# Expert rows gated at the store and gathered with accumulating transfers into the residual, in a two-layer MoE encoder

## The chip, the core and the metric

The kernel runs on one core of one Trainium2 chip, as one launch. The metric is the device time of the launch in microseconds (us), the median of several executions.

## What is computed

Two post-norm layers on x of 512 tokens by 1024 in float32. Each layer is `h = LN(alpha*h + mixer(h))` and then `h = LN(alpha*h + MoE(h))`. The mixer of the first layer is a retention and an RG-LRU head group, that of the second a gated linear recurrence (HGRN2), whose first step is a projection to v. The MoE is what the change touches:

```python
probs = softmax(x @ router_w)                       # 16 experts in 4 groups
# every token picks one group and the top-2 experts in it; gates = their probabilities, normalised
hid = silu(xblk @ w_gate[e]) * (xblk @ w_up[e])     # 1024 -> 512
yb  = hid @ w_down[e]                               # 512 -> 1024
y   = zeros.at[buf_tok].add(yb * buf_gate)          # two gated expert rows are added for each token
h   = _layer_norm(DN_ALPHA * h + y, ln_w, ln_b)
```

## The kernel before, in words

All engines run hand-ordered programs that are joined by semaphores. SyncE (queue q1) issues the weight loads, ScalarE (queue q10) the stores of expert rows, GpSimd (queue q0) the indirect transfers. `h` holds the residual in SBUF as four tiles (t = 0 to 3) of 128 tokens by 1024. `ps` is all of PSUM, eight banks of 512.

**Routing** (`route`, VectorE): the top-2 choice gives each token two slots, `dst[:, t, k]`, k = 0 and 1, and two gates, `gts`. The slots fill ten units of 128 rows (NU = 10, the last one is LAST). VectorE builds `lane_sel` and `token_of`; TensorE multiplies them (`rows_of_slots`, L652, placed after the first ten matmuls of unit 0's gate product) and VectorE turns the result into `row_at`, the token of each slot, by which GpSimd gathers the units' input rows.

**Units** (`moe`): for each unit TensorE does a gate, an up and a down product; ScalarE copies the 128 rows of the down product from PSUM to `yo` (L1102, in the helper L970) and stores them to `slot_rows` in DRAM (L1104). The last unit's rows stay in SBUF, `y_last`. Rounds for extra units stand in the program and are skipped when routing needs none; in this execution none ran. GpSimd multiplies h by alpha early in the MoE (`h_scaled`).

**End of a MoE.** When the ninth unit's rows are in DRAM (`y_stored`), GpSimd issues eight indirect gathers (L1872) of 128 rows by 4 KB, two for each tile, into the buffers `Yg`. VectorE (`norm_moe`) waits for a tile's two gathers, and adds each to h with its gate (L1471, L1473; `merged`). TensorE then sums each tile in PSUM: h through an identity matrix (L776) and the last unit's rows through the gated selection matrix `last_selT` (L781; `summed`). VectorE takes the statistics of a tile (L1413 to L1416), ScalarE the root (L1080), VectorE scales and shifts (L1427, L1431).

**After the first MoE** the v projection (L827) needs two things: the transposed tiles of h, and the two 2 MB halves of its weights, `w_v1`, which SyncE loads (L410) once the last tile's gathers have landed (`gathered[NT - 1]` at 32). TensorE waits for both halves before its first matmul. **After the second MoE** the normed tiles are stored as the output.

Of the kernel before, what the change touches and what calls it, by code (L numbers as in the profile page):

```python
# [15 lines left out]
ALU = mybir.AluOpType  # L16
# [3 lines left out]
P = 128  # L20
# [100 lines left out]
def encoder_kernel(nc, x, w_in_even, w_out_even, lru_conv_w, lru_conv_b, lru_gate_w, lru_gate_b,  # L121
# [3 lines left out]
    with ExitStack() as ctx:  # L125
# [20 lines left out]
        gts = sb("gts", [P, NT, 2])  # L146
        tbl = sb("tbl", [1, 32], I32)
# [75 lines left out]
        in_unit, past, token_of, lane = (scratch[:, 2048 + 80 * n:2128 + 80 * n] for n in range(4))  # L223
        yo = [scratch[:, 2048 + 1024 * n:3072 + 1024 * n] for n in range(2)]
        Yg = [[W3(20480, NT, D), W3(12288, NT, D)], [S3(8192, NT, D), S3(0, NT, D)]]
# [26 lines left out]
        r_rel, r_in, r_f1, r_first = (r_(2 * NT) for _ in range(4))  # L252
        r_lg = r_x
        last_sel = rt[:, 0:T].rearrange("p (t n) -> p t n", t=NT)
        last_selT, last_tmp = rt[:, T:2 * T], rt[:, T:T + P]
# [31 lines left out]
        h_scaled, merged, summed = sem("h_scaled"), sem("rows_merged"), sem("last_rows_summed")  # L287
# [44 lines left out]
        def _(sp):  # L332
# [44 lines left out]
            def moe_loads(L):  # L377
# [78 lines left out]
        def _(pe):  # L456
# [167 lines left out]
            def moe(L):  # L624
# [13 lines left out]
                def turned_extra_rows(j):  # L638

                    pe.wait_ge(extra_sel[L], j * 3 + 3)  # L640
# [327 lines left out]
        def _(act):  # L968
# [113 lines left out]
            def moe(L):  # L1082
# [13 lines left out]
                def store(b, k, stores=None):  # L1096

                    if stores is not None:
                        act.wait_ge(y_stored[L][k], stores)
                    for half in range(2):  # L1100
                        act.wait_ge(down_mm[L], b * 2 + half + 1)
                        copy(yo[k][:, half * 512:(half + 1) * 512], ps[:, 2 + half, :]).then_inc(y_copied[L], 1)  # L1102
# [12 lines left out]
                sigmoid(1)  # L1115
                store(0, 0)
# [7 lines left out]
                for half in range(2):  # L1124
                    act.wait_ge(down_mm[L], LAST * 2 + half + 1)
                    copy(y_last[:, half * 512:(half + 1) * 512], ps[:, 2 + half, :]).then_inc(y_copied[L], 1)
                act.wait_ge(table_done, 2 * L + 2)
                rounds = act.value_load(tbl[0:1, T_ROUNDS:T_ROUNDS + 1], min_val=0, max_val=ROUNDS)
                with act.Fori(0, ROUNDS, 1) as r:
                    with act.If(r < rounds):  # L1130
                        with act.Fori(0, PER_ROUND, 1) as i:
                            j = r * PER_ROUND + i
                            sigmoid(j + NU)
                            store(j + NU, 0, (j + NU // 2) * 16)
# [106 lines left out]
        def _(dve):  # L1241
# [163 lines left out]
            def tile_of(n, t):  # L1405

                halves = h[:, t, :].rearrange("p (a n) -> p a n", a=2)
                return halves, ps[:, 2 * t:2 * t + 2, :] if n % 2 else halves
# [56 lines left out]
            def norm_moe(L):  # L1465

                for t in range(NT):
                    dve.wait_ge(gathered[t], (L + 1) * 32)
                    if t == 0:
                        dve.wait_ge(h_scaled, L + 1)  # L1470
                    done(v.scalar_tensor_tensor(h[:, t, :], Yg[L][t // 2][:, 2 * (t % 2), :], gts[:, t, 0:1], h[:, t, :],  # L1471
                                                ALU.mult, ALU.add))
                    v.scalar_tensor_tensor(h[:, t, :], Yg[L][t // 2][:, 2 * (t % 2) + 1, :], gts[:, t, 1:2], h[:, t, :],  # L1473
                                           ALU.mult, ALU.add).then_inc(merged, 1)
                for t in range(NT):
                    dve.wait_ge(summed, L * NT + t + 1)
                    statistics(2 * L + 1, t)
# [454 lines left out]
```

## Time and profile before

| what | value |
|---|---|
| median of 3 runs | 1285.65 us (1285.23 to 1286.3) |
| span of the profiled execution | 1281.6 us |
| TensorE busy / VectorE busy | 96% / 41% of the span |
| chain that ended last | PE 79%, DMA 10%, DVE 7% |
| end of the first MoE, from the first gather's issue to the first v matmul | 504.43 to 535.75 us |
| end of the second MoE, from the first gather's issue to the end of the span | 1240.20 to 1281.6 us |

The profile is of one execution, whose own device time is not listed beside its span; the span is 4.05 us less than the median of the runs, which lies around it (launch and end). A busy share is an average over stages; the chain says which work ended last in each.

### The profile page before, as it was taken

How to read it: one execution, taken by the hardware profiler on the slowest of the kernel's cores; microseconds unless marked ns; L12 is line 12 of the kernel's file. 1: busy time of each engine (PE TensorE's matmuls, PEld its weight loads, DVE VectorE, ACT ScalarE, POOL GpSimd, SP SyncE). 2: the span in 40 equal slices, each digit the busy share in tenths (PEclk: the TensorE clock that was granted, in tenths of full speed). 3: DMA queues.
4: the chain of work that ended last, by engine and by line, in shares of the span. 5: the costliest groups of instructions: out<-in, count | busy, mean ns of one | idle time of the engine just before them, and what ended most of it. 6: DMA issues, size and time to landing. Idle time of an engine off the chain costs nothing.

```text
span 1281.6 us, 13883 instructions
## 1 busy us (share of the span) xinstructions
PE 1229.9 (96%) x5503; PEld 572.1 (45%) x5503; DVE 524.5 (41%) x1028; ACT 187.3 (15%) x315; POOL 168.5 (13%) x129
## 2 busy tenths in 40 slices
PE   8999999989999998999999999999899899999995
PEld 4444465443333333444555555555454433333332
DVE  1542693472211110700465766566625822111118
ACT  0016510110000000111111111111112200000000
POOL 0000310004000001000122323233310040000020
PEclk9999999999999999999999999999999999999998
DMA  9900074269999999553220122100045699999993
GB/s 355 359 1 0 1 279 185 94 265 368 425 428 426 429 428 423 223 146 131 66 66 17 50 66 65 50 15 1 1 176 250 263 411 422 430 425 429 426 415 125
DMA packets 77233, 292.62 MB, mean 228 GB/s; under 512 B 6420, under 2 KB 46200, under 8 KB 64760
## 3 DMA queue, kind: packets, MB, share of 16 engines
q1 hardware_dynamic: 59872, 257.30, 50.5%
q10 hardware_dynamic: 12408, 16.67, 3.6%
q0 software_dynamic: 4896, 17.83, 3.6%
q8 instruction: 43, 0.70, 0.2%
q14 instruction: 14, 0.11, 0.0%
HBM read 269.24 MB, written 22.54 MB: 228 GB/s over the span
## 4 chain that ended last, share of the span: by engine, by line
PE 79%; DMA 10%; DVE 7%; issue 1%; POOL 1%; ACT 1%; DVEq 0%; SPq 0%; POOLq 0%
PE ps L673 16%; PE ps L840 15%; PE ps L502 11%; PE ps L708 9%; PE ps L579 7%; PE ps L827 4%; PE ps L862 4%; DMA W<-moe_w_up 4%; PE ps L892 2%; DMA slot_rows<-hT 2%; DMA W<-moe_w_gate 2%; PE ps L629 1%; DVE S L1756 1%; PE ps L728 1%; PE ps L571 1%
## 5 line engine op out<-in xcount | busy, mean ns | idle before, releaser
L673 PE MATMUL ps<-W,S 128*64 128x512 f32 (+1 forms) x1200 | 272.8, 594 | 3.5 <-ACT S L970 1.5
L840 PE MATMUL ps<-hT,W 128*128 128x512 f32 x512 | 232.6, 593 | 0.7 <-ACT W L970 0.7
L673 PE MATMUL ps<-S 128*32 128x512 f32 (+1 forms) x592 | 140.4, 593 | 3.6 <-DMA W<-moe_w_gate 2.5
L673 PEld LDWEIGHTS ps<-W,S 128*64 128x64 f32 (+1 forms) x1200 | 82.9, 123 | 132.5 <-issue 129.0
L840 PEld LDWEIGHTS ps<-hT,W 128*128 128x128 f32 x512 | 92.9, 191 | 90.3 <-issue 88.4
L708 PE MATMUL ps<-W,hT 128*64 128x512 f32 (+1 forms) x512 | 116.6, 605 | 3.9 <-DVE hT L1695 2.0
L1894 POOL TENSOR_TENSOR W<-S,sq 128x256 f32<-128x256 f32 x64 | 73.5, 1148 | 159.3 <-PE ps L862 115.6
L502 PE MATMUL ps<-W,hT 128*128 128x512 f32 x192 | 86.4, 609 | 2.1 <-DMA W<-w_in_even 2.1
L708 PE MATMUL ps<-S,hT 128*32 128x512 f32 (+1 forms) x384 | 86.6, 599 | 1.1 <-DVE hT L1695 1.1
L970 ACT ACTIVATE hT<-ps 128x512 f32<-128x512 f32 x68 | 39.0, 598 | 330.3 <-PE ps L708 238.5
L1798 DVE TENSOR_TENSOR S<-S 128x512 f32<-128x512 f32 x64 | 47.8, 747 | 68.1 <-PE ps L862 56.3
L862 PEld LDWEIGHTS ps<-S,W 128*128 128x128 f32 x448 | 61.3, 192 | 30.1 <-issue 30.1
L1851 POOL DMA_INDIRECT S<-token_rows,row_at x18 | 17.4, 967 | 398.4 <-DVE row_at L1618 199.1
L1686 DVE TENSOR_TENSOR hT<-hT,ps 128x512 f32<-128x512 f32 x20 | 13.7, 686 | 132.5 <-ACT hT L1094 132.5
L862 PE MATMUL ps<-S,W 128*128 128x128 f32 x448 | 63.5, 286 | 1.4 <-issue 0.8
L673 PEld LDWEIGHTS ps<-S 128*32 128x32 f32 (+1 forms) x592 | 41.8, 118 | 47.7 <-issue 47.3
L1691 DVE TENSOR_TENSOR hT<-hT,ps 128x512 f32<-128x512 f32 x20 | 13.8, 688 | 114.7 <-PE ps L673 114.7
L708 PEld LDWEIGHTS ps<-W,hT 128*64 128x64 f32 (+1 forms) x512 | 34.7, 126 | 55.9 <-issue 54.8
L1695 DVE COPY hT<-ps 128x512 f32<-128x512 f32 x20 | 13.8, 690 | 110.8 <-PE ps L697 110.8
L579 PE MATMUL ps<-S 128*128 128x512 f32 x128 | 57.7, 594 | 1.0 <-DVE S L1734 1.0
L502 PEld LDWEIGHTS ps<-W,hT 128*128 128x128 f32 x192 | 37.2, 196 | 47.8 <-issue 45.3
L970 ACT ACTIVATE W<-ps 128x512 f32<-128x512 f32 x56 | 32.6, 597 | 172.6 <-PE ps L871 46.0
(276 smaller groups left out, 1350.9 us busy)
## 6 DMA issues: line engine op xcount, KB each, us to landing
W<-moe_w_gate SPq DMA_DIRECT2D x24, 2048.0 KB, 18.6
W<-moe_w_up SPq DMA_DIRECT2D x21, 2048.0 KB, 22.7
W<-moe_w_down SPq DMA_DIRECT2D x20, 2048.0 KB, 25.9
S<-moe_w_down SPq DMA_DIRECT2D x12, 2048.0 KB, 24.9
S<-moe_w_up SPq DMA_DIRECT2D x11, 2048.0 KB, 22.2
S<-moe_w_gate SPq DMA_DIRECT2D x8, 2048.0 KB, 20.9
W<-w_in_odd SPq DMA_DIRECT2D x32, 512.0 KB, 6.3
slot_rows<-hT ACTq DMA_DIRECT2D x18, 512.0 KB, 10.5
```

What stands on the lines that cost most here:

```text
L502: last = pe.matmul(ps[:, 4 + n % 4, :], a, b, start=(c == 0), stop=(c == ND - 1))
L579: last = pe.matmul(ps[:, k, :], srcT[:, c, t * P:(t + 1) * P], w[:, c, half * 512:(half + 1) * 512], start=(start and c == tiles[0]), stop ...
L673: last = pe.matmul(ps[a:a + n, bank, :], xgT[:, c, a:a + n], home(kind, p)[:, c, :], start=(c == 0), stop=(c == ND - 1))
L708: last = pe.matmul(ps[a:a + n, 2 + half, :], hidT[:, c, a:a + n], home(DOWN, p)[:, c, half * 512:(half + 1) * 512], start=(c == 0), stop=( ...
L827: last = pe.matmul(ps[:, k, :], hT[:, c, t * P:(t + 1) * P], w_v1[c // 4][:, c % 4, (k % 2) * 512:(k % 2 + 1) * 512], start=(c == 0), stop ...
L840: last = pe.matmul(ps[:, f % 2, :], ring[slot][:, f, c, :], hT[:, c, :], start=(c == 0), stop=(c == ND - 1))
L862: last = pe.matmul(o, km[level % 2][:, c * P:(c + 1) * P], mixed(Q2, s, c * P, P), start=True, stop=True)
L892: last = pe.matmul(ps[:, 7, :], vh[:, j, :], attn[:, j, :], start=(j == 0), stop=(j == NT - 1))
L970: return nc.scalar.activation(o, i, ACT.Copy)
L1798: v.tensor_tensor(q, q, view(src, at + 1, [[2, n], [step - 1, 2], [0, s]]), ALU.mult).then_inc(updated, 1)
L1851: pool.indirect_dma_start(xg[u % 3], None, token_rows, bass.IndirectOffsetOnAxis(ap=row_at[:, u:u + 1], axis=0)).then_inc(xg_in[u % 3], 16)
L1894: pool.tensor_tensor(view(km[level % 2], s, [[4 * s, m], [s, 2], [1, s]]), view(K2, s, [[4 * s, m], [T + s, 2], [1, s]]), view(ones, 0, [[ ...
```

## The change

- GpSimd no longer gathers into buffers. Each of the eight transfers adds the rows that it reads in DRAM to a tile of `h` in SBUF (`compute_op=ALU.add`). The order is k = 0 for the four tiles, then k = 1 for the four; before a tile's second transfer GpSimd waits until its first has landed.
- The rows must therefore be gated when they are stored: ScalarE's copies get a scale per row, `gate_at`, which comes out of `rows_of_slots` as ten more columns (`held_by` holds tokens and gates). So VectorE computes the gates `gts` ahead of the selection matrices and not behind them.
- VectorE's eight merging operations are gone. In the second MoE TensorE waits for a tile's transfers and sums as before. In the first MoE TensorE only sums the last unit's rows, and VectorE adds that from PSUM to h.
- SyncE loads the first half of the v weights when the last tile's first transfer has landed, and the second half when its second has.
- The selection of the last unit's rows (`last_gates`, now `last_rows`) holds ones, and takes 9 operations of VectorE where it took 22.

```diff
@@ weights of the v projection (SyncE, first layer)
                     sp.wait_ge(gate_mm[0], NU)
-                    sp.wait_ge(gathered[NT - 1], 32)
                     for half in range(2):
+                        sp.wait_ge(gathered[NT - 1], 16 * (half + 1))
                         sp.dma_start(w_v1[half], w_in_odd[0][half * 512:half * 512 + 512, D:2 * D].rearrange(rows, p=P)
                                      ).then_inc(wout_in, 16)
@@ rows_of_slots (TensorE)
-                        last = pe.matmul(ps[:, 7, 0:NU], lane_sel[:, k, :], token_of[:, k * NU:(k + 1) * NU],
+                        last = pe.matmul(ps[:, 7, 0:2 * NU], lane_sel[:, k, :], held_by[:, k * 2 * NU:(k + 1) * 2 * NU],
                                          start=(k == 0), stop=(k == 2 * NT - 1))
@@ last sums (TensorE)
                 for t in range(NT):
-                    pe.wait_ge(merged, L * NT + t + 1)
                     if t == 1:
                         pe.wait_ge(y_copied[L], copies)
-                    for half in range(2):
-                        pe.matmul(ps[:, 2 * t + half, :], ident, h[:, t, half * 512:(half + 1) * 512],
-                                  start=True, stop=False)
+                    if L == 1:
+                        pe.wait_ge(gathered[t], 64)
+                        for half in range(2):
+                            pe.matmul(ps[:, 2 * t + half, :], ident, h[:, t, half * 512:(half + 1) * 512],
+                                      start=True, stop=False)
                     if t == 0:
                         pe.wait_ge(y_copied[L], 2 * NU)
                     for half in range(2):
                         last = pe.matmul(ps[:, 2 * t + half, :], last_selT[:, t * P:(t + 1) * P],
-                                         y_last[:, half * 512:(half + 1) * 512], start=False, stop=True)
+                                         y_last[:, half * 512:(half + 1) * 512], start=(L == 0), stop=True)
@@ store and the last unit's copies (ScalarE)
+                def gated(o, i, u):
+                    return nc.scalar.activation(o, i, ACT.Copy, scale=gate_at[:, u:u + 1])
...
-                        copy(yo[k][:, half * 512:(half + 1) * 512], ps[:, 2 + half, :]).then_inc(y_copied[L], 1)
+                        gated(yo[k][:, half * 512:(half + 1) * 512], ps[:, 2 + half, :], b if extra is None else NU
+                              ).then_inc(y_copied[L], 1)
...
+                act.wait_ge(slots_done, 2 * L + 2)
                 store(0, 0)
@@ norm_moe (VectorE)
+                if L == 0:
+                    dve.wait_ge(h_scaled, 1)
                 for t in range(NT):
-                    dve.wait_ge(gathered[t], (L + 1) * 32)
-                    if t == 0:
-                        dve.wait_ge(h_scaled, L + 1)
-                    done(v.scalar_tensor_tensor(h[:, t, :], Yg[L][t // 2][:, 2 * (t % 2), :], gts[:, t, 0:1], h[:, t, :],
-                                                ALU.mult, ALU.add))
-                    v.scalar_tensor_tensor(h[:, t, :], Yg[L][t // 2][:, 2 * (t % 2) + 1, :], gts[:, t, 1:2], h[:, t, :],
-                                           ALU.mult, ALU.add).then_inc(merged, 1)
-                for t in range(NT):
+                    if L == 0:
+                        dve.wait_ge(gathered[t], 32)
                     dve.wait_ge(summed, L * NT + t + 1)
+                    if L == 0:
+                        halves, _ = tile_of(1, t)
+                        done(v.tensor_tensor(halves, ps[:, 2 * t:2 * t + 2, :], halves, ALU.add))
                     statistics(2 * L + 1, t)
@@ route (VectorE)
                 ins.then_inc(slots_done, 1)
+                for k, (d, slot) in enumerate(slots):
+                    done(v.tensor_tensor(by_token(r_rk), by_token(d), per_token(slot), ALU.is_equal))
+                    done(v.tensor_tensor(r_rk, r_rk, r_x, ALU.mult))
+                    done(v.tensor_reduce(gts[:, :, k], by_token(r_rk), AX.X, ALU.add))
...
                 dve.wait_ge(cum_ps, 2 * L + 2)
+                v.tensor_copy(gate_at[:, 0:NU], ps[:, 7, NU:2 * NU])
                 v.tensor_copy(row_at[:], ps[:, 7, 0:NU]).then_inc(slots_done, 1)
-                for k, (d, slot) in enumerate(slots):
-                    done(v.tensor_tensor(by_token(r_rk), by_token(d), per_token(slot), ALU.is_equal))
-                    done(v.tensor_tensor(r_rk, r_rk, r_x, ALU.mult))
-                    done(v.tensor_reduce(gts[:, :, k], by_token(r_rk), AX.X, ALU.add))
@@ the gathers (GpSimd)
                 pool.wait_ge(y_stored[L][0], stores)
-                for t in range(NT):
-                    for k in range(2):
-                        pool.indirect_dma_start(Yg[L][t // 2][:, 2 * (t % 2) + k, :], None, xs,
-                                                bass.IndirectOffsetOnAxis(ap=dst[:, t, k:k + 1], axis=0)
-                                                ).then_inc(gathered[t], 16)
+                pool.wait_ge(h_scaled, L + 1)
+                for k in range(2):
+                    for t in range(NT):
+                        if k == 1:
+                            pool.wait_ge(gathered[t], 32 * L + 16)
+                        pool.indirect_dma_start(h[:, t, :], None, xs,
+                                                bass.IndirectOffsetOnAxis(ap=dst[:, t, k:k + 1], axis=0),
+                                                compute_op=ALU.add).then_inc(gathered[t], 16)
```

On GpSimd, at the end of the first MoE, the rows before (names in brackets are the semaphores waited for; `tbl` is the table of rounds):

```order
L1851 DMA S<-token_rows,row_at 128x1024 [waits xgT_in_psum_0] x6
L1866 TENSOR_LOAD tbl [waits table_done]
L1866 ISA x2
L1872 DMA W<-slot_rows,dst 128x1024 [waits y_stored0_0,y_stored0_1]
L1872 DMA W<-slot_rows,dst 128x1024 x7
L1878 MEMSET S 128x512 [waits v_copied]
```

and now:

```order
L1877 TENSOR_LOAD tbl [waits table_done]
L1877 ISA x2
L1886 DMA h<-slot_rows,dst 128x1024 [waits h_scaled,y_stored0_0,y_stored0_1]
L1886 DMA h<-slot_rows,dst 128x1024 x3
L1886 DMA h<-slot_rows,dst 128x1024 [waits gathered_0]
L1886 DMA h<-slot_rows,dst 128x1024 [waits gathered_1]
L1886 DMA h<-slot_rows,dst 128x1024 [waits gathered_2]
L1886 DMA h<-slot_rows,dst 128x1024 [waits gathered_3]
```

The eight transfers stand at the same place; the last four have got a wait each for the first transfer of the same tile.

On VectorE, in `route`, between the cast of the slots and the rows that TensorE's `rows_of_slots` waits for, before:

```order
L1591 CAST dst<-S 128x4 x2
L1598 SCALAR_TENSOR_TENSOR hT<-iota,S 128x80
L1600 TENSOR_SCALAR hT<-hT 128x80
L1601 SCALAR_TENSOR_TENSOR hT<-hT 128x80
L1602 TENSOR_TENSOR hT<-hT 128x80
L1603 TENSOR_REDUCE hT<-hT 128x8
L1604 TENSOR_TENSOR S<-iota,hT 128x1024
L1606 TENSOR_TENSOR hT<-hT,iota 128x80
```

and now, first behind the cast:

```order
L1606 CAST dst<-S 128x4 x2
L1609 TENSOR_TENSOR S<-S 128x64
L1610 TENSOR_TENSOR S<-S 128x64
L1611 TENSOR_REDUCE gts<-S 128x4
L1609 TENSOR_TENSOR S<-S 128x64
L1610 TENSOR_TENSOR S<-S 128x64
L1611 TENSOR_REDUCE gts<-S 128x4
L1617 SCALAR_TENSOR_TENSOR hT<-iota,S 128x80
```

and then at the end of that stretch:

```order
L1621 TENSOR_TENSOR hT<-hT 128x80
L1622 TENSOR_REDUCE hT<-hT 128x8
L1623 TENSOR_TENSOR S<-iota,hT 128x1024
L1627 TENSOR_TENSOR hT<-hT,iota 128x8x10
L1627 TENSOR_TENSOR hT<-hT,gts 128x8x10
L1630 TENSOR_SCALAR sm<-S 128x8
```

Seven operations more stand ahead of the semaphore `sel_done` that TensorE waits for: six that make the gates, and the product with them.

## Rows read from the trace of the kernel before

**Rows 1.** The page: its span, its first line by engine, its chain by engine.

```profile
span 1281.6 us, 13883 instructions
...
PE 1229.9 (96%) x5503; PEld 572.1 (45%) x5503; DVE 524.5 (41%) x1028; ACT 187.3 (15%) x315; POOL 168.5 (13%) x129
...
PE 79%; DMA 10%; DVE 7%; issue 1%; POOL 1%; ACT 1%; DVEq 0%; SPq 0%; POOLq 0%
```

**Rows 2.** Chain that ended last, in order of time: start us, us, what.

```profile
513.20 9.13 DMA W<-slot_rows,dst
522.84 12.87 DMA W<-w_in_odd
535.75 7.13 PE ps L827 x16
```

**Rows 3.** Timeline, end of the first MoE: start us, us, engine, line, operation.

```profile
504.43 0.95 POOL L1872 DMA_INDIRECT W<-slot_rows,dst  x1 [96.44 <-DMA slot_rows<-hT]
...
510.06 1.09 PE L708 MATMUL ps<-W,hT 128*64 128x512 f32 x1 [1.93 <-DMA S<-moe_w_down]
...
522.40 0.94 SPq L410 DMA_DIRECT2D W<-w_in_odd  x2
```

**Rows 4.** DMA queues, 507 to 508 and then 508 to 522.5 us: packets, MB, share.

```profile
q1 hardware_dynamic: 88, 0.39, 96.4%
...
q0 software_dynamic: 1152, 4.19, 72.6%
q1 hardware_dynamic: 159, 0.57, 10.0%
```

**Rows 5.** Stretches: length, busy us of PE, PEld, DVE, ACT, POOL, granted clock, DMA share, GB/s.

```profile
508.00:519.00 11.00, 9.07 (x35) 3.09 (x34) 4.87 (x5) 0.75 (x2) 4.74 (x5) 0.84 1.00 399
524.00:534.00 10.00, 9.62 (x29) 4.55 (x27) 6.76 (x12) 0.99 (x3) 0.00 (x0) 1.00 1.01 394
510.00:513.50 3.50, 3.44 (x10) 1.14 (x11) 0.00 (x0) 0.00 (x0) 2.59 (x4) 0.51 1.03 410
```

**Rows 6.** Timeline, end of the second MoE and the last norm.

```profile
1240.20 0.95 POOL L1872 DMA_INDIRECT S<-slot_rows,dst  x1 [96.47 <-DMA slot_rows<-hT]
...
1252.64 1.98 PE L776 MATMUL ps<-h,sq 128*128 128x512 f32 x4
...
1254.47 1.88 PE L781 MATMUL ps<-S 128*128 128x512 f32 x4
...
1260.19 1.29 DVE L1413 BATCH_NORM_STATS2 sm<-ps 128x6 f32<-128x512 f32 x2
...
1264.77 1.29 DVE L1413 BATCH_NORM_STATS2 sm<-ps 128x6 f32<-128x512 f32 x2
```

**Rows 7.** DMA queue q1, 1241 to 1242 and then 1242 to 1257 us.

```profile
q1 hardware_dynamic: 89, 0.43, 105.4%
...
q1 hardware_dynamic: 162, 0.57, 9.4%
```

**Rows 8.** Timeline of the routing, first layer (two rows) and second layer.

```profile
284.03 0.24 DVE L1606 TENSOR_TENSOR hT<-hT,iota 128x80 f32<-128x80 f32 x1
...
286.90 1.95 PE L652 MATMUL ps<-hT,S 128*128 128x10 f32 x16
...
1019.63 0.23 DVE L1606 TENSOR_TENSOR hT<-hT,iota 128x80 f32<-128x80 f32 x1
...
1020.81 1.95 PE L652 MATMUL ps<-hT,S 128*128 128x10 f32 x16
...
1025.69 0.35 SPq L366 DMA_DIRECT2D W<-moe_w_gate  x1
```

**Rows 9.** Single lines: durations in ns, min/median/max; then indirect DMA to landing.

```profile
L1217 ACT ACTIVATE S<-ps,sm x8: 672/687/714, 962.3 to 994.1; 128x512 f32<-128x512 f32 x8
...
L1427 DVE SCALAR_TENSOR_TENSOR h<-ps,sm,S x8: 1265/1266/1267, 527.0 to 1276.0; 128x1024 f32<-128x1024 f32 x8
...
DMA to landing us min/median/max: 5.8/7.3/9.2
```

More of the change, by code:

```diff
@@ L222, in encoder_kernel @@
         first_rows = scratch[:, 3072:4096]
-        in_unit, past, token_of, lane = (scratch[:, 2048 + 80 * n:2128 + 80 * n] for n in range(4))
+        in_unit, past, lane = (scratch[:, 2048 + 80 * n:2128 + 80 * n] for n in range(3))
+        held_by = scratch[:, 2288:2448]
         yo = [scratch[:, 2048 + 1024 * n:3072 + 1024 * n] for n in range(2)]
-        Yg = [[W3(20480, NT, D), W3(12288, NT, D)], [S3(8192, NT, D), S3(0, NT, D)]]
         y_last = xg[1]
@@ L251, in encoder_kernel @@
         r_blk = r_gt[:, 0:MAXX * NE]
-        r_rel, r_in, r_f1, r_first = (r_(2 * NT) for _ in range(4))
+        r_rel, r_f1, r_first = (r_(2 * NT) for _ in range(3))
         r_lg = r_x
         last_sel = rt[:, 0:T].rearrange("p (t n) -> p t n", t=NT)
-        last_selT, last_tmp = rt[:, T:2 * T], rt[:, T:T + P]
+        last_selT = rt[:, T:2 * T]
         T_ROUNDS, T_STORES, T_COPIES, T_ORDER = MAXX, MAXX + 1, MAXX + 2, 16
@@ L638, in turned_extra_rows @@
                 def turned_extra_rows(j):
-                    pe.wait_ge(extra_sel[L], j * 3 + 3)
+                    pe.wait_ge(extra_sel[L], j * 4 + 1)
+                    for t in range(NT):
+                        for k, sel in enumerate((first_sel, other_sel)):
+                            last = pe.matmul(ps[:, 7, 0:1], sel[:, t, :], gts[:, t, k:k + 1],
+                                             start=(t == 0 and k == 0), stop=(t == NT - 1 and k == 1))
+                    last.then_inc(extra_gates[L], 1)
+                    pe.wait_ge(extra_sel[L], j * 4 + 4)
                     for half in range(2):
@@ L1094, in sigmoid, with store @@
                     nc.scalar.activation(sig, ps[:, 0, :], ACT.Sigmoid).then_inc(sig_done[L], 1)
-                def store(b, k, stores=None):
+                def gated(o, i, u):
+                    return nc.scalar.activation(o, i, ACT.Copy, scale=gate_at[:, u:u + 1])
+                def store(b, k, stores=None, extra=None):
                     if stores is not None:
                         act.wait_ge(y_stored[L][k], stores)
+                    if extra is not None:
+                        act.wait_ge(extra_sel[L], extra * 4 + 3)
                     for half in range(2):
                         act.wait_ge(down_mm[L], b * 2 + half + 1)
-                        copy(yo[k][:, half * 512:(half + 1) * 512], ps[:, 2 + half, :]).then_inc(y_copied[L], 1)
+                        gated(yo[k][:, half * 512:(half + 1) * 512], ps[:, 2 + half, :], b if extra is None else NU
+                              ).then_inc(y_copied[L], 1)
                     act.wait_ge(y_copied[L], b * 2 + 2)
@@ L1125, in moe @@
                     act.wait_ge(down_mm[L], LAST * 2 + half + 1)
-                    copy(y_last[:, half * 512:(half + 1) * 512], ps[:, 2 + half, :]).then_inc(y_copied[L], 1)
+                    gated(y_last[:, half * 512:(half + 1) * 512], ps[:, 2 + half, :], LAST).then_inc(y_copied[L], 1)
                 act.wait_ge(table_done, 2 * L + 2)
@@ L1133, in moe @@
                             sigmoid(j + NU)
-                            store(j + NU, 0, (j + NU // 2) * 16)
+                            store(j + NU, 0, (j + NU // 2) * 16, extra=j)
             norm_std(0, 0)
@@ L1705, in moe @@
                     if u == 1:
-                        last_gates(L)
+                        last_rows(L)
                     elif u == 4:
-                        last_gates_turned(L)
+                        last_rows_turned(L)
                     elif L == 0 and u == 6:
@@ L1869, in moe @@
                 pool.wait_ge(y_stored[L][0], stores)
[L1870 to L1874 removed]
+                pool.wait_ge(h_scaled, L + 1)
+                for k in range(2):
+                    for t in range(NT):
+                        if k == 1:
[3 more added lines that the diff above has]
+                                                compute_op=ALU.add).then_inc(gathered[t], 16)
             moe(0)
```

44 lines of the change are left out of this document (20 added, 24 removed).

## The prediction, made before the changed kernel ran

> **What bounds the kernel now.** I read the page first: TensorE is busy for 96% of the span and holds 79% of the chain that ended last [rows 1]. So only what moves TensorE's start or end counts. The chain in order of time shows the two places that the change touches. At the end of the first MoE it leaves TensorE: last gather (513.20, landed 522.33), loads of the v weights (second half issued 522.84, landed 535.71), v projection at 535.75 [rows 2]. The first v matmul waits for weights, which wait for gathers; VectorE's merging is not on that path. At the end of the second MoE the chain is the gathers and then VectorE: the last norm starts at 1260.19 and each of its four tiles takes 4.58 us (1260.19 to 1264.77) [rows 6]. The third place is the routing of the second layer, where the first load of new weights is issued at 1025.69, when unit 0's gate product is done [rows 8].
>
> Then I read the queues. The first gather is issued at 504.43 and none of its bytes move before 508; 0.57 MB of weights are still to come then, and the eight gathers move 4.19 MB [rows 3, 4]. From 508 to 519 the DMA share is 1.00 at 399 GB/s [rows 5]: the transfers are bound by the DMA engines, not by GpSimd's issue (0.95 us each). One gather of 0.524 MB costs c = 0.524 / 0.399 = 1.31 us of all 16 engines. 508.1 + 0.57/0.399 (1.4) + 8 x 1.31 = 520.0, and the last one counted as landed at 522.33: 2.3 us lie between last data and release.
>
> **The change, part by part.**
>
> *The accumulating transfer* is the unknown. No row shows one. It writes the same bytes as a gather, but it must also read the tile of h. Lower bound: that read is hidden and c stays 1.31 us (factor 1). Upper bound: the read takes the engines as long as the gather itself, so c = 2.62 us (factor 2); the engines are at 1.00 already [rows 5], so there is no idle share to take it in. I take 1.5, the middle: half of the second read hidden behind the write, c = 1.96 us. I know nothing from the trace that says which half; both ends stay for the range.
>
> The Trainium skill, "Collectives: The Full Stack", section "The bandwidth ceiling: the fold count and why AG ≠ RS ≠ AR", speaks against this change: an add in the DMA engine costs no time itself, but needs two source reads on one ring, and it runs at half the rate of a copy. By that rule the factor is 2, and the sum below would be +15.3 us instead of +6.2. No run here shows it yet.
>
> *First MoE's end, factor 1.5.* The four k = 0 transfers end at 508.1 + 1.4 + 4 x 1.96 = 517.4 and are released at 519.7. SyncE then issues half 0 of the v weights. The loads cost 5.3 us of data a half (2.1 MB at 394 GB/s [rows 5]); of the 13.3 us from 522.40 to 535.71 [rows 2, 3] 10.6 are data, and I split the other 2.7 into 1.2 before and 1.5 after. So half 0 starts moving at 520.9. At that time 7.9 - 3.5 = 4.4 us of k = 1 transfers are left (they queue behind the k = 0 ones, so their waits cost nothing while the queue is full). Both move packet by packet: 4.4 x (1 + 1/1.5) = 7.3 us together, k = 1 ends at 528.1, counted at 530.4. Half 1 starts at 531.6, ends at 536.9, and the first v matmul is at 538.4, against 535.75: **+2.7**. With factor 1 the same steps give 514.7, 517.0, 518.2, 521.7, 530.6 and 532.1 (-3.7); with factor 2, 544.2 (+8.5).
>
> *The clock.* Without the identity matmuls TensorE ends its sums near 523, does eight short transposes, and then stands idle until the v projection. Before, after a short burst and a wait of 1.93 us at 510.06 [rows 3], the granted clock was 0.51 for 3.5 us [rows 5], the lower of the two levels, and 3.5 us did the work of 1.8. I add **+1.7**, whatever the factor, since the idle time is over 3 us in each case. First place: +4.4 (factor 1: -2.0; factor 2: +10.2).
>
> *Hidden there:* VectorE's new adds from PSUM cost 1.27 us a tile (as L1427, which reads 1024 columns of PSUM [rows 9]). Tile 0 has landed by about 522, and add, norm and transposes need some 8 us, so it is ready near 530, before the weights. If that cover were gone it would cost 1.3. The eight merges (1.28 each) go, and gain nothing here.
>
> *Second MoE's end.* First bytes at 1242.1 (q1 alone before), 0.57 MB of weights left [rows 7]. k = 0 ends at 1242.1 + 1.4 + 7.9 = 1251.4, tile 0's second transfer at 1253.3, released 1255.6. TensorE is free from 1252.64 on and needs 3.7 us for tile 0 (1252.64 to 1254.47 + 1.88 [rows 6]); it has stood 3 us idle, so +1.7: 1261.1. VectorE starts there, not at 1260.19: **+1.0**. From then on the tiles come every 2 us and VectorE needs 4.58, so it sets the end as before. Factor 1: released 1252.3, so tile 0's sums end when TensorE allows, 1256.35, **-3.8** and no clock loss; factor 2: +4.3.
>
> *Routing.* Seven operations of about 0.25 us stand ahead of what L652 waits for: +1.8. First layer: ready at 284.27 + 1.8 = 286.1, needed at 286.90: hidden with 0.8 to spare. Second layer: 1019.86 + 1.8 + 0.1 = 1021.7, needed at 1020.81: 0.8 to 0.9 late [rows 8]. Behind L652 stands the rest of unit 0's gate product, and SyncE's loads at 1025.69 wait for its end; so **+0.8** passes to the end. The ten more columns are under 0.1 us.
>
> *At nothing:* the scaled copies (0.69 against 0.60 us, by L1217 [rows 9]), since ScalarE's copies are needed a unit later, and for the last unit 0.2 us hide behind the transfers; the smaller `last_rows` and the wait of `store` for `slots_done`, long past; the extra rounds, which don't run.
>
> **Sum:** +4.4 + 1.0 + 0.8 = **+6.2 us**. The profiled execution's span is 1281.6; it becomes 1287.8, and with the 4.05 us between span and median, **1291.9 us**.
>
> **The rivals.**
>
> *A. The add is free (factor 1).* For it: the second read is from SBUF, another memory than the one that feeds the gather. Against: the engines' share of 1.00. Time: -2.0 - 3.8 + 0.8 = -5.0, 1280.7 us: faster. It decides below a factor of about 1.25, where the three terms are +1.3 - 2.3 + 0.8 = -0.2.
>
> *B. Factor 2.* c = 2.62; +10.2 + 4.3 + 0.8 = +15.3, 1301.0 us. For it: two reads for one write on engines that are already busy. The Trainium skill's page on collectives, cited above, states this case.
>
> *C. Worse than double:* packets that wait for their own read of h. With factor 3 the steps give +21.3 + 10.8 + 0.8 = +33, 1318.6 us. Nothing in the trace speaks for it, since gathers run packets back to back.
>
> *D. It cancels:* a factor of 1.15 to 1.35, within 0.2%.
>
> **How the numbers follow.** Forecast (factor 1.35 to 1.8) 0.36; A 0.34; B 0.12; C 0.06; D 0.12. About 0.2% (2.6 us) is what a measurement of this kernel can tell from no change. Faster by more is A, 0.34; within is D, 0.12; slower is the rest, 0.54. Both signs hold much, so the range goes from A to B, 1280 to 1301 us; that of the likeliest case alone is 1288 to 1298.
>
> **What would show it.** In the profile after: the landing time of the transfers (before 5.8 to 9.2 us [rows 9]) and the rate of q0 while DMA is full, 399 GB/s with A, some 270 with the forecast, 200 with B; the first v matmul at 538 (532, 544), at granted clock 0.5; the second norm's first statistics 1.8 us later than before (3.0 earlier with A); L652 of the second layer 0.8 us later. It is wrong if the k = 1 transfers do not queue behind the k = 0 ones, if half 0 takes more than its share from them, or if the clock holds.

## The result

The changed kernel takes 1300.41 us (median of 4 runs, 1296.61 to 1303.83), the kernel before 1285.44 us beside it. The ratio is 1.0123, 95% interval 1.0102 to 1.0144: slower by 15 us. The changed kernel's four executions lie in two pairs, 1296.61 and 1297.01 and then 1303.81 and 1303.83, so its median falls between them, and the profile (span 1302.0 us) is of one of the upper pair.

The page of the changed kernel has the span, the engines and, in its third part, the queue that carries the indirect transfers (packets, MB, time as a share of 16 engines):

```profile
span 1302.0 us, 13820 instructions
...
PE 1231.0 (95%) x5487; PEld 571.9 (44%) x5487; DVE 504.5 (39%) x994; ACT 191.1 (15%) x315; POOL 177.5 (14%) x129
...
q0 software_dynamic: 4896, 17.83, 5.1%
```

VectorE is busy for 20 us less than in [rows 1] and TensorE 1.1 us longer. Neither explains the result. The last line does: the kernel before has the same packets and MB on q0 with 3.6% in the last column. The same bytes occupy the DMA engines longer: 5.1% of 1302.0 is 66 us, 3.6% of 1281.6 is 46 us, some 1.3 us more for each of the sixteen transfers.

The chain that ended last, at the two places of the change (start us, us, what; rows of `issue`, all under 0.3 us, are left out):

```profile
511.27 11.63 DMA h<-slot_rows,dst
523.16 13.14 DMA h<-slot_rows,dst
536.32 7.86 DMA W<-w_in_odd
544.22 9.71 PE ps L835 x16
...
1254.90 8.31 DMA h<-slot_rows,dst
1263.47 10.21 DMA h<-slot_rows,dst
1273.81 3.75 PE ps L784 x4
1277.57 2.95 PE ps L789 x4
1280.54 1.31 DVE sm L1429 x2
```

Against [rows 2], one gather of 9.13 us ahead of the v weights has become two transfers, 24.8 us together. The v weights' second half now lands 7.86 us after the last of them instead of 12.87, because the load overlaps the transfers. The first v matmul is at 544.22 instead of 535.75. At the second end the chain now goes through two transfers of tile 0 and then through TensorE's sums to the norm. Before, it went through one gather and then through VectorE's merges, again without `issue`:

```profile
1246.46 8.67 DMA S<-slot_rows,dst
1255.16 1.30 DVE h L1471
1256.48 1.28 DVE h L1473
1257.76 1.21 DVE h L1471
1258.99 1.28 DVE h L1473
1260.28 1.22 DVE sm L1413 x2
```

So 5.1 us of VectorE's merging lay on the path at this end, and they are gone now.

The timeline of GpSimd and SyncE there (first and last row GpSimd, then SyncE's v weights):

```profile
505.64 1.60 POOL L1886 DMA_INDIRECT h<-slot_rows,dst  x1 [96.23 <-DMA slot_rows<-hT]
...
514.91 1.55 POOL L1886 DMA_INDIRECT h<-slot_rows,dst  x1 [2.09 <-DMA h<-slot_rows,dst]
...
523.16 1.55 POOL L1886 DMA_INDIRECT h<-slot_rows,dst  x1 [0.91 <-DMA h<-slot_rows,dst]
...
522.97 13.73 SPq L411 DMA_DIRECT2D W<-w_in_odd  x2
```

The transfers of k = 0 are issued at 505.64 to 511.27. The first of k = 1 has to wait for a landing (2.09 us), and the last is issued at 523.16; before, the last gather was issued at 513.20 [rows 2]. The stretches show whether the issue or the engines limit this (length, busy us of PE, PEld, DVE, ACT, POOL, granted clock, DMA share, GB/s):

```profile
514.00:520.00 6.00, 5.13 (x22) 1.97 (x19) 0.00 (x0) 1.38 (x2) 3.10 (x2) 1.00 1.06 214
520.00:526.00 6.00, 5.65 (x14) 2.19 (x12) 0.54 (x1) 1.28 (x1) 3.11 (x2) 1.00 1.07 213
544.00:549.00 5.00, 4.78 (x6) 2.18 (x7) 1.80 (x5) 0.00 (x0) 0.00 (x0) 0.50 0.00 0
1273.00:1277.00 4.00, 3.19 (x4) 1.51 (x5) 0.00 (x0) 0.00 (x0) 0.00 (x0) 0.51 1.06 209
```

The DMA share is 1.06 to 1.07 while only 213 to 214 GB/s are moved: the engines are full with half of the bytes. Before it was 399 GB/s [rows 5], so **the factor is 399 / 213 = 1.9**, and a transfer of 0.524 MB costs 0.524 / 0.2135 = 2.45 us of all 16 engines where a gather cost 1.31, 1.14 more. GpSimd issues one per 1.85 us, so it isn't the limit. The factor is near the 2 of the Trainium skill ("Collectives: The Full Stack", section "The bandwidth ceiling: the fold count and why AG ≠ RS ≠ AR"), which has a reduction's adding step run at half the rate of a copy; the page measured it on a ring of several cores, and this is an ordinary gather on one. The two last rows show the lower of the two clock levels (0.50, 1.2 of 2.4 GHz) at the first v matmuls, after 10.82 us in which TensorE waited for the weights, and at the second end's sums, after 6.15 us of wait.

The spans differ by 20.4 us, the medians by 15.0. Each run's time is 1.8 us over its span, so the profiled execution before was 2.0 us under its median and the changed one 3.4 over. In the profiles the way goes like this: first gather 1.2 later; from it to the first v matmul 38.6 us instead of 31.3 (**+7.3**); first part of the v projection (its 16 matmuls and the transposes behind them, until the next part starts) 10.42 us instead of 7.84 (**+2.6**, the clock); the product by which TensorE picks the first unit's rows out of h in the second layer (L728, now L735) 10.17 instead of 7.13 us (+3.0); second end from first gather to the norm's first statistics 25.6 instead of 20.0 us (**+5.65**). The +1.2 and +3.0 lie in products that the change doesn't touch. This first rows' product took 8.83 us in the first layer (granted clock 0.81) and 7.13 in the second (1.00) before, and 10.04 and 10.17 after (0.71 and 0.70). It takes 7.13 in both layers of e5 and e6, and 8.83 and 8.65 in e9, which are the changed kernel in that part, so I don't count it to the change; with the +1.2 it makes most of the 5 us between the two differences. The three bold terms are 15.6 us. That this is so near to 15.0 is partly luck, with executions in two pairs 7 us apart.

### The profile page after: what moved, and what is told of

It reads as the page before. It is cut to its first block, busy times and chain, and to the rows that moved or that the text cites. A ratio compares the mean times of both kernels' runs of the same rounds, so it can differ in the third digit from the quotient of the medians.

```text
span 1302.0 us, 13820 instructions
## 1 busy us (share of the span) xinstructions
PE 1231.0 (95%) x5487; PEld 571.9 (44%) x5487; DVE 504.5 (39%) x994; ACT 191.1 (15%) x315; POOL 177.5 (14%) x129
## 4 chain that ended last, share of the span: by engine, by line
PE 81%; DMA 10%; DVE 7%; issue 1%; ACT 1%; POOL 0%; DVEq 0%; SPq 0%; POOLq 0%
PE ps L680 17%; PE ps L848 15%; PE ps L503 11%; PE ps L715 9%; PE ps L580 7%; PE ps L835 4%; PE ps L870 4%; DMA h<-slot_rows,dst 3%; PE ps L900 2%; DMA W<-moe_w_up 2%; DMA slot_rows<-hT 2%; DMA W<-moe_w_gate 2%; PE ps L735 2%; PE ps L630 1%; DVE S L1767 1%
## 5 line engine op out<-in xcount | busy, mean ns | idle before, releaser
L503 PE MATMUL ps<-W,hT 128*128 128x512 f32 x192 | 85.2, 602 | 3.1 <-DMA W<-w_in_even 3.1
L835 PE MATMUL ps<-W,hT 128*128 128x512 f32 x128 | 58.3, 615 | 10.8 <-DMA W<-w_in_odd 10.8
L1106 ACT ACTIVATE hT<-ps,gate_at 128x512 f32<-128x512 f32 x36 | 24.7, 687 | 234.9 <-PE ps L715 234.9
## 6 DMA issues: line engine op xcount, KB each, us to landing
slot_rows<-hT ACTq DMA_DIRECT2D x18, 512.0 KB, 10.4
```

The costliest lines, as they stand in the source:

```text
L503: last = pe.matmul(ps[:, 4 + n % 4, :], a, b, start=(c == 0), stop=(c == ND - 1))
L835: last = pe.matmul(ps[:, k, :], hT[:, c, t * P:(t + 1) * P], w_v1[c // 4][:, c % 4, (k % 2) * 512:(k % 2 + 1) * 512], start=(c == 0), stop ...
```

## The experiments

Times of the kernel before, run beside the experiments, had medians of 1284.02 (e1 to e4), 1285.15 (e5 to e8) and 1283.58 us (e9); the ratios compare fast runs as recorded, and differ from the quotients of these medians by up to 0.2%. Each distance from a profile is of one execution, and it can differ without an edit to the transfers: the first end is 36.9 us in e4 and 38.6 in the changed kernel, whose transfers and weight loads are the same. "First end" is first gather's issue to first v matmul (31.3 before, 38.6 after); "second end" is first gather's issue to the norm's first statistics (20.0 and 25.6).

| kernel | median us | ratio [95%] | first end | first part of v | second end |
|---|---|---|---|---|---|
| e1 transfers overwrite | 1282.92 | 0.9998 [0.998, 1.0016] | 29.9 | 9.43 | 16.4 |
| e2 gated rows, plain gathers | 1284.27 | 1.0000 [0.9987, 1.0013] | 31.1 | 7.84 | 20.0 |
| e3 adding transfers in second MoE only | 1290.72 | 1.0040 [1.0024, 1.0056] | 31.0 | 7.85 | 24.8 |
| e4 TensorE kept busy | 1296.61 | 1.0094 [1.0067, 1.0120] | 36.9 | 7.74 | 23.8 |
| e5 only k = 1 adds | 1287.36 | 1.0035 [1.0016, 1.0053] | 35.4 | 9.69 | 17.3 |
| e6 v weights not by halves | 1304.46 | 1.0158 [1.0135, 1.0181] | 41.9 | 9.59 | 26.8 |
| e7 before, v weights first | 1277.27 | 0.9947 [0.9926, 0.9968] | 23.1 | 9.54 | 19.6 |
| e8 before, longer hold ahead of the router | 1284.93 | 0.9993 [0.9975, 1.0011] | 30.9 | 9.54 | 20.4 |
| e9 after, v weights first | 1288.60 | 1.0039 [1.0023, 1.0055] | 27.05 | 10.71 | 24.9 |

### e1: the changed kernel, transfers that overwrite

```diff
                         pool.indirect_dma_start(h[:, t, :], None, xs,
-                                                bass.IndirectOffsetOnAxis(ap=dst[:, t, k:k + 1], axis=0),
-                                                compute_op=ALU.add).then_inc(gathered[t], 16)
+                                                bass.IndirectOffsetOnAxis(ap=dst[:, t, k:k + 1], axis=0)
+                                                ).then_inc(gathered[t], 16)
```

> The changed kernel with its sixteen transfers as plain gathers into h (no add): the sums of the MoE and the residual are left out, all waits and all other instructions stay. Theory (the add makes the DMA engines read twice, some 1.9 times the engine time of a gather): the queue's rate while DMA is full goes back from 213 to about 400 GB/s, the first v matmul comes some 27 to 28 us after the first transfer's issue and not 38.6, the second norm some 18 us after it and not 25.6, and the time falls by 15 to 20 us to 1280 to 1285. Rival (the waits for the first transfer of a tile and the order k = 0, k = 1 cost the time): both distances keep more than half of their growth, and the time stays above 1294.

The kernel leaves out the residual and the sum of the expert rows. Without the add, the time is that of before. All waits, the order and the halves are still those of the changed kernel, so the loss is the add's. The two distances missed the expectation: the first end is 29.9 us and not 27 to 28, the second 16.4 and not 18. Lines of e1: GpSimd's issues (ns, min/median/max) with their landing times, and a stretch:

```profile
L1886 POOL DMA_INDIRECT h<-slot_rows,dst x16: 950/952/952, 504.6 to 1253.0; - x16
...
DMA to landing us min/median/max: 5.1/7.3/9.5
...
510.00:514.00 4.00, 3.34 (x10) 1.16 (x12) 0.00 (x0) 0.00 (x0) 0.95 (x1) 0.57 1.02 406
```

406 GB/s again, and issues of 0.95 us. What the add does inside the engine isn't shown: packets and bytes of q0 are the same with it and without, so a second read is the likely reading and no more. The same lines of the changed kernel:

```profile
L1886 POOL DMA_INDIRECT h<-slot_rows,dst x16: 1546/1554/1596, 505.6 to 1271.4; - x16
...
DMA to landing us min/median/max: 8.9/10.4/13.1
```

e1 also bounds what the rest of the change is worth. The second end is 3.6 us shorter than before and the first 1.4, of which 1.6 are lost again in the first part of v. If the add were free, the change would still have gained only about 1 us by the medians (0.2 to 0.3 by the ratio), an amount that the interval (0.998 to 1.0016) doesn't tell from nothing.

### e2 and e3: the change without its transfers, and with them in one place

In both, rows are stored gated. e2 gathers them into buffers, and VectorE adds without a gate; e3 does so in the first MoE alone. The v weights wait as before where gathers are plain.

```diff
+        PLAIN = (0, 1)          # e3: (0,)
...
-                        sp.wait_ge(gathered[NT - 1], 16 * (half + 1))
+                        sp.wait_ge(gathered[NT - 1], 32 if 0 in PLAIN else 16 * (half + 1))
...
+                if L in PLAIN:
+                    for t in range(NT):
+                        dve.wait_ge(gathered[t], (L + 1) * 32)
+                        done(v.tensor_tensor(h[:, t, :], Yg[L][t // 2][:, 2 * (t % 2), :], h[:, t, :], ALU.add))
+                        v.tensor_tensor(h[:, t, :], Yg[L][t // 2][:, 2 * (t % 2) + 1, :], h[:, t, :], ALU.add
+                                        ).then_inc(merged, 1)
```

> Rows gated at the store, but gathered into buffers by plain transfers as before, added by VectorE without a gate, and the v weights loaded as before: what is left of the change is the routing's new order and the scaled copies. Theory: within 1 us of the kernel before in both ends, the second layer's routing at most 0.9 us later, so 1285 to 1287. Rival (the gates on the store's path or the seven operations in routing cost several us): 1289 or more.

> Accumulating transfers in the second MoE alone, the first as in the kernel before. Theory: the first end costs about 10 us of the change (7 by transfers and weights, 2.6 by the clock of the v projection), the second about 5.6, so this run is at 1290 to 1293. Rival (the loss is mostly at the second end): 1296 or more.

e2 is the kernel before in time: gates at the store, the longer routing ahead of `rows_of_slots` and the scaled copies cost nothing that can be measured. Its profile still shows the routing term: `rows_of_slots` starts 15.0 us after the first rows' product in the second layer instead of 14.2 (+0.8, as forecast), and at 286.99 instead of 286.90 in the first.

e3 shows the second end alone: +4.8 us in the profile (24.8 against 20.0), and 6.7 us by the medians or 5.1 by the ratio. Its timeline has the same picture as the changed kernel's, TensorE idle for a landing and then VectorE late:

```profile
1261.76 3.75 PE L790 MATMUL ps<-h,sq 128*128 128x512 f32 x4 [7.96 <-DMA h<-slot_rows,dst]
1265.31 2.13 PE L795 MATMUL ps<-S 128*128 128x512 f32 x4
...
1267.47 0.70 DVE L1435 BATCH_NORM_STATS2 sm<-ps 128x6 f32<-128x512 f32 x1 [21.72 <-PE ps L795]
```

### e4: the clock

```diff
@@ last sums (TensorE)
+                if L == 1:
+                    spin(0, 7)
@@ ahead of the v projection (TensorE)
+            pe.wait_ge(ln_done, NT + 2)
+            spin(2, 7)
             pe.wait_ge(wout_in, 48)
```

> The changed kernel with seven idle matmuls on TensorE while it waits for the v weights, and seven while it waits for the second MoE's first tile; nothing else waits for them. Theory (TensorE's clock has fallen by the time the wait ends, which costs 2.6 us in the v projection and about 3 in the first tile's sums): the first v tile's matmuls take 7.1 us and not 9.7, tile 0's sums 3.7 and not 6.7, and the time is 4 to 6 us under the changed kernel's. Rival (the clock does not follow from the idle time): no change, 1299 to 1301.

`spin` issues matmuls that nobody reads. The v projection then ran at full clock:

```profile
544.00:549.00 5.00, 5.00 (x14) 2.25 (x13) 1.46 (x4) 0.00 (x0) 0.00 (x0) 1.00 0.00 0
```

The first part of v took 7.74 us (10.42 without): the clock's share there is real, and it comes back whole. At the second end it doesn't:

```profile
1268.91 3.27 PE L786 MATMUL ps<-h,sq 128*128 128x512 f32 x4 [2.52 <-DMA h<-slot_rows,dst]
...
1274.35 1.29 DVE L1433 BATCH_NORM_STATS2 sm<-ps 128x6 f32<-128x512 f32 x2 [20.01 <-PE ps L791]
```

TensorE stands idle for 2.52 us behind the idle matmuls, at a granted clock of 0.68 from 1268 to 1272, and tile 0's sums take 5.44 us to the statistics, where 3.7 were expected and 6.73 were needed without. The end is 1.9 us shorter. The median fell by 3.8 us, a little less than the 4 to 6 expected; with four executions of each kernel the two intervals overlap, so it is the profile and not the times that shows the clock's share. The transfers' share stays: 1.0094.

### e5: half of the adds

```diff
+                        add = {"compute_op": ALU.add} if k == 1 else {}
                         pool.indirect_dma_start(h[:, t, :], None, xs,
                                                 bass.IndirectOffsetOnAxis(ap=dst[:, t, k:k + 1], axis=0),
-                                                compute_op=ALU.add).then_inc(gathered[t], 16)
+                                                **add).then_inc(gathered[t], 16)
```

> The changed kernel with the add in the second transfer of each tile alone; the first one overwrites the tile, so the residual and, in effect, one part of the sum are left out. Theory (each add costs engine time, 2.6 us a transfer for 1.3): with four adds at each end in place of eight the first v matmul comes 33 to 36 us after the first transfer's issue (38.6 with eight, 29.9 with none), the second norm 16 to 19 us after it (25.6 and 16.4, since only tile 0's one add lies on the path), and the time is 1286 to 1290. Rival (a fixed price for mixing adds and copies, or the clock): as with eight, 1296 or more.

The loss follows the number of adding transfers on the path. At the second end tile 0 needs five transfers before its sums: four of k = 0 and its own of k = 1. In e5 one of the five adds, so 1.14 us are due over e1; it is 17.3 against 16.4. In the changed kernel all five do: 5.7 us, and 3.0 for the clock that falls, so 8.7 are due; measured are 25.6 - 16.4 = 9.2. At the first end four more adds (4.6 us due) give 35.4 - 29.9 = 5.5, and eight (9.1 due) give 8.7. One price of 1.14 us a transfer explains the four numbers within 1 us. Such distances differ by up to 1.7 us without an edit to the transfers (e4), so that each add costs the same is not shown more closely than that.

GpSimd's issue follows the add too (0.947 us the shortest in e5, 1.590 the longest), in one program and on one line:

```profile
L1887 POOL DMA_INDIRECT h<-slot_rows,dst x16: 947/1249/1590, 501.3 to 1257.6; - x16
```

### e6: the halves undone

```diff
                     for half in range(2):
-                        sp.wait_ge(gathered[NT - 1], 16 * (half + 1))
+                        sp.wait_ge(gathered[NT - 1], 32)
```

> The changed kernel with the v weights waiting for all transfers, as in the kernel before: the loading by halves undone. Theory (the halves fill queue time that the weights need anyway, and push the second transfers back by as much): the first v matmul comes about 2 us later than with halves, 40 to 41 us after the first transfer's issue, and the time is 1 to 3 us over the changed kernel's. Rival (the first half gets in the way of the adds and the halves cost more than they save): the same or faster.

The first end is 3.4 us longer than in the changed kernel, where about 2 were expected, and the median 4.1. The times show less than the medians say: one execution is at 1297.89 and four are at 1303.69 to 1304.93, where the changed kernel has two at 1297 and two at 1303.8, so like groups differ by about 1 us, and the two intervals overlap. The halves were a gain at the first end by this profile; how much of it the whole time keeps is open.

### e7: the kernel before, with the v weights ahead of half of the gathers

If the first v matmul waits for weights that are queued behind bytes that are needed later, the order is what can be gained. This kernel starts from the one before. Its gathers are plain, and SyncE no longer waits for them.

```diff
                     sp.wait_ge(gate_mm[0], NU)
-                    sp.wait_ge(gathered[NT - 1], 32)
...
                 for t in range(NT):
+                    if L == 0 and t == 2:
+                        pool.wait_ge(wout_in, 48)
                     for k in range(2):
                         pool.indirect_dma_start(Yg[L][t // 2][:, 2 * (t % 2) + k, :], None, xs,
...
+                    if L == 0:
+                        merge(t)
                     dve.wait_ge(summed, L * NT + t + 1)
+                    if L == 0:
+                        halves, _ = tile_of(1, t)
+                        done(v.tensor_tensor(halves, ps[:, 2 * t:2 * t + 2, :], halves, ALU.add))
```

`merge(t)` is the two gated adds of one tile, so that VectorE merges, sums and norms tile by tile; TensorE sums only the last rows, as in the changed kernel.

> The kernel before, with plain gathers and its gates, and three edits at the first MoE's end: the v weights are loaded as soon as the last gate product is done, GpSimd holds back the gathers of tiles 2 and 3 until they have landed, and VectorE merges and norms tile by tile and adds the last unit's rows itself. Theory (the v projection waits for two weight halves and one tile only, so bytes for the other tiles should go last): weights landed at 526 to 528, the first v matmul at 528 to 530 and not 535.75, the clock held since TensorE is busy until 526, and the time 5 to 7 us under the kernel before. Rival (the held-back tiles come too late or the clock falls): under 2 us gained.

1277.27 us, 0.9947 [0.9926, 0.9968]: **faster than both kernels**, and by 7.9 us under the one before where 5 to 7 were expected. The three edits were made together, so the gain is that of the order with the tile-by-tile merging. Its timeline (SyncE's loads, two of GpSimd's gathers, the first v matmul):

```profile
500.56 0.94 SPq L409 DMA_DIRECT2D W<-w_in_odd  x2
...
505.31 0.95 POOL L1887 DMA_INDIRECT W<-slot_rows,dst  x1 [96.53 <-DMA slot_rows<-hT]
...
528.59 0.98 POOL L1887 DMA_INDIRECT W<-slot_rows,dst  x1 [18.57 <-DMA W<-w_in_odd]
...
528.37 8.83 PE L827 MATMUL ps<-W,hT 128*128 128x512 f32 x16 [0.99 <-DMA W<-w_in_odd]
```

The loads are issued 22 us earlier than in [rows 3], and the first end is 23.1 us instead of 31.3. TensorE now waits 0.99 us for weights. 1.7 us go back to the clock (first part of v 9.54 us, at a granted clock of 0.63 from 528.4 to 533), which was expected to hold.

### e8: the clock ahead of the router

```diff
-            spin(1, 6)
+            spin(1, 9)
```

in both layers, in the kernel before.

> The kernel before with nine idle matmuls in place of six ahead of the router's counts, in both layers. Theory (the 3 us by which single executions differ at that place are TensorE's clock, which falls or not with how long TensorE stands idle there): the product that gathers the first rows takes 7.1 us in both layers and never 8.8 to 10, and the time is 1 to 3 us under the kernel before, with less spread. Rival (the idle matmuls delay the counts): the same or slower.

The first rows' product took 7.13 us in both layers, as expected, but the time didn't fall: 0.9993 [0.9975, 1.0011], and runs still spread from 1281.19 to 1288.85. In its profile the first part of v took 9.54 us instead. That the router's clock explains the spread between runs was my reading of the profile pair, and as a statement on times it fell. What decides where the clock falls from run to run stays open.

### e9: the changed kernel, with the v weights ahead of half of the transfers

```diff
-                        sp.wait_ge(gathered[NT - 1], 16 * (half + 1))
...
-                for k in range(2):
-                    for t in range(NT):
+                order = [(t, k) for p in (0, 2) for k in range(2) for t in (p, p + 1)] if L == 0 else [
+                    (t, k) for k in range(2) for t in range(NT)]
+                for n, (t, k) in enumerate(order):
+                    if L == 0 and n == 4:
+                        pool.wait_ge(wout_in, 48)
```

> The changed kernel, but in the first MoE the v weights are loaded as soon as the last gate product is done, as in e7, and the accumulating transfers come by pairs of tiles: those of tiles 0 and 1 at once, those of tiles 2 and 3 when the v weights have landed. It tells whether the loss at the first MoE's end comes from the bytes' order or from the rate. Theory (the add halves the transfers' rate, whoever is queued behind them): four accumulating transfers ahead of or among the weights keep the engines 4.6 us longer than four plain ones (4 x (2.45 - 1.31)), and the weights land up to that much later than in e7: first gather to first v matmul 25 to 28 us (23.1 in e7, 38.6 in the changed kernel). Tile 2 is then late: its three transfers need 7.4 us and 2.3 of release after the issue, its add, norm and transposes some 8, so the v projection's third tile waits 2 to 5 us. The second end keeps its 25.6 us. Time: 1300.4 - 12 + 3.5, some 1288 to 1294, slower than before. Rival (the loss at the first end is only the order of bytes, and an add costs little while weights stream beside it): first v matmul as in e7, 23 to 24 us, no wait at the third tile, and 1277.3 + 5.6 = 1283.

The time is in the theory's range and not the rival's, and so is the first end (27.05). The second is 24.9 us, 0.7 under the 25.6 expected. A part of the expectation missed: the v projection's third tile didn't wait, since a tile of v takes some 14 us, not 7. The chain shows what the first v matmul waits for now, with the rows between left out, and below it the transfer that GpSimd holds back until the weights have landed:

```profile
508.33 9.18 DMA h<-slot_rows,dst
517.77 9.65 DMA h<-slot_rows,dst
527.50 1.24 DVE h L1490
528.75 1.30 DVE sm L1428 x2
...
532.12 1.30 DVE h L1446
...
535.38 10.00 PE ps L834 x16
...
534.15 1.55 POOL L1889 DMA_INDIRECT h<-slot_rows,dst  x1 [10.86 <-DMA W<-w_in_odd]
```

Tile 0's two transfers follow one another, 9.18 and 9.65 us, since the second must not start before the first has landed; then come VectorE's add and norm. In e7, whose gathers needn't wait for each other, VectorE merged tile 0 at 516.46, 11.15 us after the first issue (19.2 us here to the add). The weights are later too: they have landed 25.8 us after the first issue, against 23.0 in e7.

## Why the prediction was off

The direction was right. The time, 1300.41, lies in the range, at its upper edge, and 8.5 us above the forecast of 1291.9: the case that came true is rival B (1301.0), which had a chance of 0.12.

- **The step that failed** is "I take 1.5, the middle: half of the second read hidden behind the write, c = 1.96 us". The factor is 1.9 and c is 2.45 us. Its own argument for the upper bound was the better one: the engines stood at a share of 1.00, which left no idle share to take more work in. While DMA is full 213 GB/s are moved, where the forecast said some 270 and B 200. e1 and e5 show that the add alone makes the factor. With 2.45 in place of 1.96 the prediction's own steps give +7.1 for the transfers and weights, +3.3 at the second end, and +12.9 in all instead of +6.2. So this one term is 6.7 of the 8.8 us that were missed.
- **First end.** +2.7 was forecast for the transfers and weights, +8.5 with factor 2, for a first v matmul at 544.2. It stood at 544.22, of which 1.2 were there before the first transfer: +7.3 from the gathers on. The steps of that sum (release, split of the loads) held: with 2.45 us a transfer they give +7.1. That the matmul stood at the very time of factor 2 is luck, since 1.2 us of it came from ahead. The halves gain 3.4 us in e6's profile, which the prediction had in its steps without naming it.
- **The clock** was a right mechanism with too small a size. +1.7 was forecast at each of two places; it was +2.6 at the v projection (e4 takes it back whole) and some 3 at the second end, where the sums took 6.73 us from 1273.81 to the statistics against 3.7 at full clock (e4 takes back 1.3 of it). Its reason, the length of the wait, doesn't carry alone: v's first part took 7.84 or 7.85 us behind waits of 1.68 to 2.13 us (before, e2, e3) and 9.43 to 10.42 behind waits of 4.17 to 13.98 (e8, e1, e5, changed, e6), but also 9.54 and 10.71 in e7 and e9, whose last waits were 0.99 and 0.79 us.
- **Second end.** +1.0 was forecast, +4.3 with factor 2; it was +5.65. Tile 0's second transfer was released 18.8 us after the first issue, and the steps with factor 2 give 18.7, with 2.45 us a transfer 17.9; the 0.9 us between are open. The rest is the clock. (The steps with factor 2 end at +4.1 and not +4.3, which changes nothing.)
- **Routing** +0.8: right, shown in e2 (15.0 against 14.2 us), too small for the times to show. In the changed kernel's own profile it isn't there: `rows_of_slots` starts 17.2 us after the first rows' product, 3.0 more than before, just what the product itself took longer, so the seven operations were hidden behind it. Hidden in the first layer: right.
- **VectorE's adds** (1.23 us each, 1.27 forecast) are hidden as said: tile 0's was at 525.46, its norm and transposes ended at 533.4, eleven us before the weights. The scaled copies cost nothing: right (e2).
- **Rival A** (1280.7, the add is free) is what e1 tries. Its time, 1282.92, is 2.2 above A's. Its second end is right (-3.6 of -3.8) and so is the clock at the first (+1.6 of +1.7), but the first v matmul came only 1.4 us earlier, not 3.7.
- Of what would make it wrong, "if the k = 1 transfers do not queue behind the k = 0 ones" came half true. In e1 GpSimd issues the last transfer of k = 0 at 508.4 and the first of k = 1 only at 512.7, behind a landing; I take this for what A's first end lacks, without a run of its own. In the changed kernel the waits are 0.90 to 2.09 us, and the engines stay full under them, so they cost little.
- **Rival B** had the right mechanism. Its sum (+15.3) is nearer than its terms: it has +10.2, +4.3 and +0.8 where the profile shows 9.9, 5.65 and nothing, and the errors cancel.

## What to carry to other kernels

An add in a transfer isn't free where the DMA engines are the limit. Look at their share in the stretch concerned: here it was 1.00, and a transfer with the add took 1.9 times the engine time. About 20 us of VectorE work, of which only 5.1 lay on the chain, were exchanged for 1.14 us more of engine time in each of sixteen transfers. Before you make a transfer at a stage's end cheaper or richer, ask which bytes the next stage needs first. In this kernel their order, with a merge tile by tile that lets the next stage start on the first tile, gave 7.9 us (e7), with the old gathers. A longer wait of TensorE can cost more behind it at the lower clock, here 1.6 to 3.0 us, so a delay on its path is to be counted with that.

## What the hardware showed unexpectedly

- GpSimd's issue of an indirect transfer takes 1.55 us with the add and 0.95 without, on the same line of one program (e5).
- The landing time grew from 5.8/7.3/9.2 us [rows 9] to 8.9/10.4/13.1. The whole of it hits a chain of dependent transfers twice (e9).
- While adding transfers alone ran, the profile's DMA share stood at 1.06 at 213 GB/s. Mixed with the v weights' plain loads it was 1.05 at 280 to 312 GB/s (e9, from 514 to 526 us), between the two rates.
- One and the same product (the first unit's rows) took from 7.13 to 10.17 us, at granted clocks of 1.00 to 0.70, in kernels that don't differ there. The wait just before it was 1.36 or 1.37 us each time.
